# Convolution taps of six channel tiles as 32-column products in four column groups, on rows that transfers lay out four times

## The chip, the cores and the metric

The kernel runs on one core of one Trainium2 chip. The metric is the device time of one execution in microseconds; the profile is one profiled execution on that core. Engines: PE (TensorE; PEld is its weight load), DVE (VectorE), ACT (ScalarE), POOL (GpSimd), SP (SyncE, which issues all DMAs here).

## What is computed

A two-layer Conformer-like model on 256 tokens with 1024 channels, then a second block with gated recurrence, attention and 16 experts. The change lies in the convolution module of the first layer:

```python
def conv_module(h, w_pw1, w_dw, g_norm, w_pw2):
    u = h @ w_pw1
    a, b = jnp.split(u, 2, axis=-1)
    u = a * jax.nn.sigmoid(b)
    u = lax.conv_general_dilated(
        u, w_dw[:, None, :].astype(u.dtype), window_strides=(1,),
        padding=[(CONV_WIDTH - 1, 0)],
        dimension_numbers=("NWC", "WIO", "NWC"),
        feature_group_count=D_MODEL)
    u = jax.nn.silu(rmsnorm(u, g_norm))
    return u @ w_pw2
```

All is float32. Each of the 1024 channels has 31 tap weights of its own: out[c, t] is the sum over w of w_dw[w, c] u[c, t + w - 30].

## The kernel before, in words

Channels lie on partitions, in KD = 8 tiles of 128; tokens lie on the free axis, T = 256. There is one program per engine, and semaphores order them; each engine works its own list strictly in order. Weights come in 1 MB slots into a ring of six; SP issues a slot's load when the product that used the place before is done (`wait_free`).

**Products in three parts** (`split_product`, `mm3`, lines 702 to 704). A weight half slot is split into a high part by ACT (`split_hi`, line 1454) and the rest by DVE (`split_lo`, line 1958), and x likewise. There are four half-slot buffers, so ACT can split a half when the half four before it has been multiplied. PE takes 24 products per half slot.

**pw1** has eight slots in pairs: the even slot of a pair makes a, the odd one b, for two channel tiles. DVE's `glu_gate` (line 2096) multiplies b by the norm's root, ACT takes the sigmoid (line 1561), GpSimd's `scale_gate` (line 1896) multiplies by the root again (for a), and DVE's `glu` (line 2088) writes the product with a into `conv_in`, whose rows have 30 zeros ahead of them. Ahead of pw1 slot 2, PE turns the rows of the small vectors and of w_dw into columns (lines 842 to 845), and DVE copies all 248 columns of tap weights into `w_dw_room` (line 2076). ACT then computes the condition's SiLU (line 1544) and goes on with the splits.

**The taps.** Tiles 0, 1, 3, 5 and 7 are summed on DVE, 31 instructions of 256 columns each (`taps`, lines 2113 and 2117), spread by hand between the splits and GLU steps of pw1 and behind them. Tiles 2, 4 and 6 are on PE: for each tap ACT scales the identity by the column of weights (`diagonals`, line 1552, a ring of 16), and PE multiplies the 128x128 diagonal by the 256 columns of `conv_in` that begin at w (`tap`, line 873): 93 products into banks 7 and 1.

**The stage between pw1 and pw2 on PE** (list in the PE program): for each of six early chunks of the modulation, `mod_product` (line 855: for each half slot four products of 32 columns of weights, in four column groups, by 512), `turn_mod` of the chunk before (line 862), and a share of the taps (`TAP_STEPS`). Behind chunk 2 come the transposes of the context rows (line 890), behind chunk 3 the sums of the context's squares (`sum_squares`, line 734), behind chunk 5 its turn, then the sums of conv_out's squares, 22 products with zeros (`KEEP_WARM`, line 900), and pw2 with four slots. ACT copies each chunk's product (line 1574), makes diagonals, copies sums of taps out of PSUM (`take_taps`, line 1567), squares and takes the roots (line 1442). DVE takes the reciprocal (line 1929), the normed tiles (line 1938) and the low parts of x (line 1950), and pw2 begins.

SP's list: pw1's eight loads, six chunks of modulation (two loads each, `mod_chunk`), pw2's four loads, and the next feed-forward block.

Of the kernel before, what the change touches and what calls it, by code (L numbers as in the profile page):

```python
# [15 lines left out]
ALU = mybir.AluOpType  # L16
# [3 lines left out]
P = 128  # L20
D = 1024
KD = D // P
T = 256
# [14 lines left out]
KEEP_WARM = 22  # L38
# [44 lines left out]
NORMS = ("ffn0", "conv_in", "context", "conv_out", "ffn1", "ffn2", "mla", "mla_q", "mla_kv", "ffn3", "tokens", "final1")  # L83
# [8 lines left out]
PE_MARKS = ("first_gains_turned", "rows_turned", "ctx_turned", "rope_turned", "ak_product", "key_dec_turned",  # L92
# [37 lines left out]
def constant_table():  # L130
# [6 lines left out]
    }  # L137

# [25 lines left out]
    parts["mask_cols"] = np.tile(np.where(p < CHUNK, 0.0, MASKED), (P, 1))  # L164
    parts["inv_freq"] = (np.float64(10000.0) ** (-2.0 * (p % (ROPE // 2)) / ROPE))[:, None]
# [25 lines left out]
def build(nc, x, positions, ffn_norm1, ffn1_w1, ffn1_w3, ffn1_w2, mix_norm, ffn_norm2, ffn2_w1, ffn2_w3, ffn2_w2,  # L191
# [15 lines left out]
    with ExitStack() as ctx:  # L207
# [32 lines left out]
        w_dw = w_dw_room[:, 0:KD * CONV_W].rearrange("p (k w) -> p k w", w=CONV_W)  # L240
# [65 lines left out]
        conv_in, conv_acc, glu_sig = r1.take(KD, PAD + T), r1.take(KD, T), r1.take(2, 2 * T)  # L306
        cond_pad, mod_rows = r1.take(KD, 32), r1.take(2, 512)

        PE_TILES, DVE_TILES = (2, 4, 6), (0, 1, 3, 5, 7)
        DIAGS = 16  # L310
        TAP_BANK = {2: (7, 0), 4: (7, T), 6: (1, 0)}
        TAPS = [(j, w) for j in PE_TILES for w in range(CONV_W)]
        TAP_STEPS = (0, 16, 32, 47, CONV_W * 2, 78, len(TAPS))
        diag = arena[:, ARENA - 16 * P:ARENA].rearrange("p (q c) -> p q c", c=P)
# [187 lines left out]
        def _(sp):  # L502
# [26 lines left out]
            def small_inputs():  # L529
                rows_in(vectors[2:])  # L530
                sp.dma_start(rows_dw, conv_w_dw[0]).then_inc(sem("rows_in"), 16)
                for j, g in enumerate((q_norm_g_2, k_norm_g_2)):
                    for half in range(2):
                        sp.dma_start(qk_gain[64 * half:64 * half + 64, j:j + 1], g.rearrange("a d -> d a")
                                     ).then_inc(sem("gains_in"), 16)
                sp.dma_start(mask_in, masks).then_inc(sem("masks_in"), 16)
                sp.dma_start(router[:, :, :], w_router_2[0].rearrange("(k p) e -> p k e", p=P)).then_inc(sem("router_in"), 16)
                sp.dma_start(pos_i[:, :], positions.partition_broadcast(P)).then_inc(sem("positions_in"), 16)
# [54 lines left out]

            for c in range(MOD_EARLY):
                mod_chunk(c)
            for j in range(4):
# [88 lines left out]
        def _(pe):  # L685
# [42 lines left out]
            def sum_squares(m, k_tiles, n, bank, first=0):  # L728
# [1892 lines left out]
```

## Time and profile before

| what | us |
|---|---|
| median of 3 runs | 1828.26 (1827.47 to 1829.78) |
| the profiled execution, its own time | 1828.54 |
| its span | 1826.7 |
| PE busy, of the span | 1668.9 (91%) |
| DVE, ACT, POOL busy | 844.6, 684.5, 10.7 |
| mean granted clock of PE, share of full speed | 0.968 |

The span runs from the first to the last instruction of the execution; the own time is 1.84 us longer. Busy time of an engine is the union of its instructions; matmuls are pipelined, so that the duration of one (from issue to modelled end) is longer than the distance from its start to the next one's. A float32 product that is not split leaves two records. "Idle before" names the instruction that ended an engine's wait.

### The profile page before, as it was taken

The page shows a single profiled execution, that of the slowest core. Times are in us where ns is not written, and L with a number is a line of the kernel's source. Part 1 is how long each engine was busy: PE and PEld are TensorE (multiplying, and loading weights), DVE is VectorE, ACT ScalarE, POOL GpSimd, SP SyncE. Part 2 cuts the span into 40 slices and gives each one's busy share as a digit, 9 for nine tenths or more (in the row PEclk, how much of TensorE's full clock was granted, in tenths as well). Part 3 has the DMA queues.
Part 4 walks back from the last instruction along what each step waited for, and adds up shares of the span by engine and source line. Part 5 has one row for each costly group of instructions (what it writes and reads, how often), then busy time and mean ns, then how long its engine had stood idle before and what let it go on. Part 6 is the DMA issues. An engine that isn't in the chain of part 4 may idle for free.

```text
span 1826.7 us, 31145 instructions
## 1 busy us (share of the span) xinstructions
PE 1668.9 (91%) x13465; PEld 1416.3 (78%) x13465; DVE 844.6 (46%) x1201; ACT 684.5 (37%) x954; POOL 10.7 (1%) x8
## 2 busy tenths in 40 slices
PE   8999999999999999999999999999999876675755
PEld 7999997899999999868999988988786432322422
DVE  6555698765557555314655564984522000000001
ACT  5444547644445444223444455756602010100101
POOL 0000020000000000000000000000000000000000
PEclk9999999999999999999999999999999998978988
DMA  9745455355555455352554352435677999999997
GB/s 293 249 163 191 151 194 198 120 185 192 185 181 176 164 191 184 113 193 89 203 184 168 131 165 95 133 106 171 268 285 302 426 426 427 427 427 426 425 427 328
DMA packets 189679, 427.50 MB, mean 234 GB/s; under 512 B 8004, under 2 KB 146678, under 8 KB 174485
## 3 DMA queue, kind: packets, MB, share of 16 engines
q1 hardware_dynamic: 189588, 426.19, 63.5%
q8 instruction: 70, 1.15, 0.3%
q14 instruction: 21, 0.16, 0.0%
HBM read 425.12 MB, written 1.05 MB: 233 GB/s over the span
## 4 chain that ended last, share of the span: by engine, by line
PE 73%; DMA 20%; DVE 5%; ACT 1%; issue 1%; SPq 0%; another core or an unknown queue 0%; DVEq 0%; ACTq 0%
PE banks L702 15%; PE banks L704 15%; PE banks L703 15%; DMA arena<-in_w_exp_gate 5%; DMA ring<-in_w_exp_gate 3%; DMA xn<-in_w_exp_up 3%; DMA h<-in_w_exp_down 3%; DMA arena<-in_w_exp_down 3%; DMA arena<-in_w_exp_up 2%; PE banks L873 2%; DMA ring<-in_w_exp_up 2%; PE banks L1084 2%; PE banks L1086 2%; PE banks L1085 2%; PE banks L1358 2%; PE banks L825 2%
## 5 line engine op out<-in xcount | busy, mean ns | idle before, releaser
L702 PE MATMUL banks<-x_split,w_split 128*128 128x256 f32 x1600 | 456.4, 285 | 9.5 <-DVE w_split L1958 3.9
L1958 DVE TENSOR_TENSOR w_split<-ring,w_split 128x1024 fp32r<-128x1024 f32 x288 | 346.4, 1224 | 237.9 <-ACT w_split L1454 237.4
L703 PE MATMUL banks<-x_split,w_split 128*128 128x256 f32 x1600 | 452.7, 283 | 0.0
L704 PE MATMUL banks<-x_split,w_split 128*128 128x256 f32 x1600 | 452.7, 283 | 0.0
L1454 ACT ACTIVATE w_split<-ring 128x1024 fp32r<-128x1024 f32 x287 | 295.2, 1051 | 190.0 <-PE banks L704 188.2
L702 PEld LDWEIGHTS banks<-x_split,w_split 128*128 128x128 f32 x1600 | 307.0, 192 | 13.3 <-issue 5.8
L703 PEld LDWEIGHTS banks<-x_split,w_split 128*128 128x128 f32 x1600 | 307.0, 192 | 0.3
L704 PEld LDWEIGHTS banks<-x_split,w_split 128*128 128x128 f32 x1600 | 307.0, 192 | 0.0
L702 PE MATMUL banks<-hid_split,w_split 128*128 128x256 f32 x704 | 199.6, 284 | 0.0
L703 PE MATMUL banks<-hid_split,w_split 128*128 128x256 f32 x704 | 199.2, 283 | 0.0
L704 PE MATMUL banks<-hid_split,w_split 128*128 128x256 f32 x704 | 199.2, 283 | 0.0
L702 PEld LDWEIGHTS banks<-hid_split,w_split 128*128 128x128 f32 x704 | 135.1, 192 | 0.6 <-DVE hid_split L2027 0.6
L703 PEld LDWEIGHTS banks<-hid_split,w_split 128*128 128x128 f32 x704 | 135.1, 192 | 0.0
L704 PEld LDWEIGHTS banks<-hid_split,w_split 128*128 128x128 f32 x704 | 135.1, 192 | 0.0
L2582 DVE TENSOR_TENSOR roots<-banks,roots 128x256 f32<-128x256 f32 x16 | 6.8, 424 | 268.7 <-PE banks L1358 268.7
L1358 PE MATMUL banks<-arena 128*32 128x256 f32 x992 | 76.2, 462 | 37.1 <-DMA arena<-in_w_exp_up 25.3
L1358 PEld LDWEIGHTS banks<-arena 128*32 128x32 f32 x992 | 35.1, 128 | 77.1 <-DMA arena<-in_w_exp_up 31.7
L1086 PE MATMUL banks<-x_hi,w_rest 128*128 128x256 f32 (+1 forms) x288 | 89.8, 312 | 0.0
L1503 ACT ACTIVATE hid_split<-gated 128x512 fp32r<-128x512 f32 x44 | 27.8, 632 | 150.3 <-DVE gated L2025 150.3
L2012 DVE TENSOR_TENSOR gated<-banks,roots 128x512 f32<-128x512 f32 x88 | 60.3, 685 | 34.2 <-PE banks L704 34.0
L2587 DVE TENSOR_TENSOR roots<-banks,arena 128x512 f32<-128x512 f32 x16 | 11.1, 691 | 138.8 <-PE banks L1364 138.8
L1084 PE MATMUL banks<-x_hi,w_gates 128*128 128x256 f32 (+1 forms) x216 | 70.5, 327 | 0.0
(411 smaller groups left out, 2260.3 us busy)
## 6 DMA issues: line engine op xcount, KB each, us to landing
ring<-in_ffn_w SPq DMA_DIRECT2D x131, 1024.0 KB, 5.1
arena<-in_w_exp_gate SPq DMA_DIRECT2D x13, 2048.0 KB, 45.0
ring<-in_w_mod SPq DMA_DIRECT2D x24, 1024.0 KB, 5.1
arena<-in_w_exp_down SPq DMA_DIRECT2D x12, 2048.0 KB, 45.2
arena<-in_w_exp_up SPq DMA_DIRECT2D x11, 2048.0 KB, 45.7
ring<-in_w_in SPq DMA_DIRECT2D x21, 1024.0 KB, 5.2
ring<-in_w_exp_down SPq DMA_DIRECT2D x9, 2048.0 KB, 45.0
ring<-in_w_exp_gate SPq DMA_DIRECT2D x7, 2048.0 KB, 46.7
```

Source lines behind the costliest of these rows:

```text
L702: mm(out_, hi, moving(0), start=start, stop=False, **kw)
L703: mm(out_, hi, moving(1), start=False, stop=False, **kw)
L704: return mm(out_, lo, moving(0), start=False, stop=stop, **kw)
L825: last = mm(ps[:, bank0 + tile // 2, (tile % 2) * T:(tile % 2) * T + T], slot(n)[:, k * half_cols + o * P:k * half_cols + o * P + P], src[ ...
L873: mm(ps[:, b, c:c + T], diag[:, q % DIAGS, :], conv_in[:, j, w:w + T], start=(w == 0), stop=(w == CONV_W - 1)).then_inc(sem("diag_used"), 1)
L1084: mm(out_, hi, x_hi[:, k, rows], start=(k == 0), stop=False)
L1085: mm(out_, hi, x_rest[:, k, rows], start=False, stop=False)
L1086: last = mm(out_, lo, x_hi[:, k, rows], start=False, stop=(k == KD - 1))
L1358: last = mm(ps[32 * q:32 * q + 32, 4 + m, 0:256], src(2 * j + k), w[:, k * D + 256 * q:k * D + 256 * q + 256], start=(j == 0 and k == 0), ...
L1454: fn(half_part(n, o, 0), half_slot(n, o, columns), ACT.Copy).then_inc(sem("half_hi"), 1)
L1958: ins = dve.tensor_tensor(half_part(n, o, 1), half_slot(n, o, columns), half_part(n, o, 0).bitcast(F32), ALU.subtract)
L2012: return dve.tensor_tensor(dst, ps[:, bank + c % 2, :].rearrange("p (k t) -> p k t", t=T), scale, ALU.mult)
```

## The change

Tiles 0 and 1 stay on DVE. Tiles 2 to 7 go to PE, two at a time. For a pair of tiles SP issues 16 SBUF to SBUF transfers (`shift_pair`): for each of four row groups g of 32 channels and each shift `first` of 0 to 3 columns, the 32 rows go to partitions 32*first, so that each group of channels lies on all 128 partitions, four times, each time a column further on. One product then does four taps of 32 channels; eight of them (m), 4 columns apart, do all 31 taps. The four groups of channels are the four column groups. DVE makes the weights, 128x1024 a tile, from a table `quad` and the tap weights (`spread_taps`); ACT lays the tap weights out as `w_tap`, in 16 small copies from PSUM. GpSimd's part goes; DVE scales both a and b by the root (`glu_scale`), and pw1's slots 4 and 6 wait for that rather than for glu. PE waits for all four glu ahead of the first modulation product. conv_out's sums go ahead of modulation product 5 and of the context's sums; the context's root moves behind conv_out's on ACT and DVE; the last turn goes between pw2 slots 1 and 2; the warming products fall from 22 to 4. `conv_acc` lies where the normed tiles will be (`xn[:, :, T:2T]`), and pairs 1 and 3 share the rows of `conv_in`. Several semaphores of small loads become one, `small_in`.

```diff
-KEEP_WARM = 22
+KEEP_WARM = 4
...
+    quad = p[:, None] % 32 == np.arange(32)[None, :]
...
-        w_dw = w_dw_room[:, 0:KD * CONV_W].rearrange("p (k w) -> p k w", w=CONV_W)
+        w_dw = w_dw_room[:, 0:2 * CONV_W].rearrange("p (k w) -> p k w", w=CONV_W)
+        w_tap = w_dw_room[:, 64:256].rearrange("p (k g m) -> p k g m", g=4, m=8)
...
+            def shift_pair(p):
+
+                sp.wait_ge(sem("glu_ready"), p + 1)
+                for first in range(4):
+                    for g in range(4):
+                        sp.dma_start(shifted[p][32 * first:32 * first + 32, :, g, :],
+                                     conv_pair(p)[32 * g:32 * g + 32, :, first:first + WIDE]
+                                     ).then_inc(sem(f"pair_shifted_{p}"), 16)
+
             for c in range(MOD_EARLY):
                 mod_chunk(c)
+                if c < 3:
+                    shift_pair(c + 1)
...
                 if j >= 4 and j % 2 == 0:
-                    pe.wait_ge(sem("glu_ready"), j // 2 - 1)
+                    pe.wait_ge(sem("glu_scaled"), j // 2 - 1)
...
+            def taps(pair):
+
+                pe.wait_ge(sem(f"pair_shifted_{pair}"), 16 * 16)
+                for a in range(2):
+                    j = 2 * pair + a
+                    pe.wait_ge(sem("taps_spread"), j - 1)
+                    for m in range(8):
+                        for g in range(4):
+                            last = mm(ps[32 * g:32 * g + 32, PAIR_BANK[pair], a * T:a * T + T],
+                                      tap_room(j)[:, g, 32 * m:32 * m + 32], shifted[pair][:, a, g, 4 * m:4 * m + T],
+                                      start=(m == 0), stop=(m == 7))
+                last.then_inc(sem("pe_mark"), 1)
...
+            pe.wait_ge(sem("cond_ready"), 1)
+            pe.wait_ge(sem("glu_ready"), KD // 2)
+            early_mod(0)
+            taps(1)
+            early_mod(1)
+            taps(2)
+            early_mod(2)
+            pe.wait_ge(sem("taps_copied"), 1)
+            taps(3)
+            early_mod(3)
             pe.wait_ge(sem("taps_copied"), 2)
+            pe.wait_ge(sem("ctx_in"), 16)
...
+            early_mod(4)
+            sum_squares("conv_out", KD, T, 7)
+            early_mod(5)
+            sum_squares("context", KD, T, 4, at=T)
+            pe.wait_ge(sem("mod_copied"), 5)
             for _ in range(KEEP_WARM):
...
             for j in range(4):
                 split_product(FIRST["pw2"] + j, j, first="pw2" if j == 0 else None)
+                if j == 1:
+                    pe.wait_ge(sem("std_ready"), NORM["context"])
+                    turn_mod(MOD_EARLY - 1, mod_rows, 4, T + 8 * (MOD_EARLY - 1))
...
+            rows = ps[:, 6, 2 * CONV_W:KD * CONV_W].rearrange("p (k w) -> p k w", w=CONV_W)
+            for first in range(4):
+                n = 8 if first < 3 else 7
+                for g in range(4):
+                    fn(w_tap[32 * first:32 * first + 32, :, g, 0:n],
+                              rows[32 * g:32 * g + 32, :, first:first + 4 * n - 3:4], ACT.Copy)
...
+            mod_copy(0, mod_rows, 5)
+            take_taps(1)
+            mod_copy(1, mod_rows, 6)
+            take_taps(2)
+            mod_copy(2, mod_rows, 5)
+            take_taps(3)
+            mod_copy(3, mod_rows, 6)
+            act.wait_ge(sem("conv_done"), 2)
+            for pair in range(4):
+                square_pair(pair)
...
+            fn(xn[:, :, 0:T], ctx_rows, ACT.Copy).then_inc(sem("ctx_copied"), 1)
+            mod_copy(4, mod_rows, 5)
+            fn(squares[:, :, T:2 * T], ctx_rows, ACT.Square).then_inc(sem("squares_ready"), 1)
+            split_hi_slot(FIRST["pw2"])
+            root("conv_out", 7, D)
...
+            def glu_scale(pair):
+
+                wait_done(dve, FIRST["pw1"] + 2 * pair + 1)
...
+                dve.tensor_tensor(glu_sig[:, pair % 2, :].rearrange("p (a t) -> p a t", t=T),
+                                  ps[:, (2 * pair + 1) % 4, :].rearrange("p (a t) -> p a t", t=T), scale, ALU.mult
+                                  ).then_inc(sem("glu_gate_scaled"), 1)
+                if pair == 3:
+                    dve.wait_ge(sem("pair_shifted_1"), 16 * 16)
+                dve.tensor_tensor(conv_pair(pair)[:, :, PAD:PAD + T],
+                                  ps[:, (2 * pair) % 4, :].rearrange("p (a t) -> p a t", t=T), scale, ALU.mult
+                                  ).then_inc(sem("glu_scaled"), 1)
...
+                dve.tensor_tensor(tap_room(j).rearrange("p g (m c) -> p g m c", c=32),
+                                  const("quad").unsqueeze(1).unsqueeze(1).to_broadcast([P, 4, 8, 32]),
+                                  w_tap[:, j - 2].unsqueeze(3).to_broadcast([P, 4, 8, 32]), ALU.mult
+                                  ).then_inc(sem("taps_spread"), 1)
...
+            glu_scale(0)
             split_lo_slot(FIRST["pw1"] + 4)
             glu(0)
             taps((0, 0, 4), (1, 0, 4))
             split_lo_slot(FIRST["pw1"] + 5)
-            glu_gate(1)
-            taps((0, 4, 8), (1, 4, 8))
+            glu_scale(1)
+            taps((0, 4, 6), (1, 4, 6))
             glu(1)
+            spread_taps(2)
+            spread_taps(3)
             split_lo_slot(FIRST["pw1"] + 6)
-            taps((0, 8, 12), (1, 8, 12))
+            taps((0, 6, 9), (1, 6, 9))
             split_lo_slot(FIRST["pw1"] + 7)
-            glu_gate(2)
-            taps((0, 12, 17), (1, 12, 17))
+            spread_taps(4)
+            glu_scale(2)
+            taps((0, 9, 11), (1, 9, 11))
             glu(2)
-            taps((0, 17, 24), (1, 17, 24))
-            glu_gate(3)
-            taps((0, 24, CONV_W), (1, 24, CONV_W), (3, 0, 6))
+            spread_taps(5)
+            taps((0, 11, 16), (1, 11, 16))
+            glu_scale(3)
+            taps((0, 16, 18), (1, 16, 18))
             glu(3)
-            taps((3, 6, CONV_W), (5, 0, 20))
-            taps((5, 20, CONV_W), (7, 0, 12))
-            taps((7, 12, CONV_W))
-            root("context", T)
+            spread_taps(6)
+            spread_taps(7)
+            taps((0, 18, CONV_W), (1, 18, CONV_W))
             split_lo_slot(FIRST["pw2"])
-            dve.wait_ge(sem("taps_copied"), len(PE_TILES))
+            dve.wait_ge(sem("taps_copied"), 3)
             normed("conv_out", x_in, conv_acc, gains("conv_norm"))
             x_lo("pw2")
             split_lo_slot(FIRST["pw2"] + 1)
+            root("context", T)
             split_lo_slot(FIRST["pw2"] + 2)
```

## Rows read from the trace of the kernel before

**Rows 1.** The page, part 4: the chain that ended last, by engine.

```profile
PE 73%; DMA 20%; DVE 5%; ACT 1%; issue 1%; SPq 0%; another core or an unknown queue 0%; DVEq 0%; ACTq 0%
```

**Rows 2.** Windows, 259 to 326: start:end, us, busy of each engine, PEclk, DMA share, GB/s.

```profile
259.00:326.00 67.00, 67.00 (x382) 50.78 (x383) 55.64 (x125) 45.04 (x99) 1.27 (x1) 1.00 0.60 201
```

**Rows 3.** Timeline of PE: start, us, engine, line, operation [idle before, releaser].

```profile
258.93 1.92 PE L855 MATMUL banks<-ring,arena 128*32 128x512 f32 x16
260.78 7.18 PE L873 MATMUL banks<-arena 128*128 128x256 f32 x32
267.89 1.92 PE L855 MATMUL banks<-ring,arena 128*32 128x512 f32 x16
269.75 1.05 PE L862 MATMUL banks<-consts,arena 128*128 128x2 f32 x8
270.66 7.16 PE L873 MATMUL banks<-arena 128*128 128x256 f32 x32
...
321.79 3.70 PE L734 MATMUL banks<-squares,consts 128*128 128x256 f32 x16
325.32 4.91 PE L900 MATMUL banks<-zero_w 128*128 128x512 bf16 x22
331.89 0.36 PE L702 MATMUL banks<-x_split,w_split 128*128 128x256 f32 x1 [1.66 <-DVE x_split L1950]
```

**Rows 4.** Timeline of PE in the experts: products of 128x32 weights.

```profile
1411.96 1.91 PE L1358 MATMUL banks<-arena 128*32 128x256 f32 x32
1413.69 1.91 PE L1358 MATMUL banks<-ring,arena 128*32 128x256 f32 x32
```

**Rows 5.** Timeline of ACT, pw1 slot 2.

```profile
220.78 0.22 ACT L1544 ACTIVATE arena<-vec_b 128x16 f32<-128x16 f32 x1 [1.25 <-DVE w_dw_room L2076]
220.91 2.94 ACT L1454 ACTIVATE w_split<-ring 128x1024 fp32r<-128x1024 f32 x3
```

**Rows 6.** Timeline of DVE in pw1 and behind it.

```profile
229.05 1.54 DVE L1958 TENSOR_TENSOR w_split<-ring,w_split 128x1024 fp32r<-128x1024 f32 x1 [1.65 <-ACT w_split L1454]
...
236.39 2.35 DVE L1958 TENSOR_TENSOR w_split<-ring,w_split 128x1024 fp32r<-128x1024 f32 x2
...
258.48 5.62 DVE L2117 SCALAR_TENSOR_TENSOR arena<-arena,w_dw_room 128x256 f32<-128x256 f32 x14
264.01 0.68 DVE L2096 TENSOR_TENSOR arena<-banks,roots 128x512 f32<-128x512 f32 x1
...
273.51 0.67 DVE L2088 TENSOR_TENSOR arena<-banks,arena 128x512 f32<-128x512 f32 x1
```

**Rows 7.** Timelines of ACT and DVE, the conv_out root up to pw2.

```profile
289.02 1.88 ACT L1583 ACTIVATE xn<-banks 128x2048 f32<-128x2048 f32 x1 [1.34 <-PE banks L890]
...
325.52 0.47 ACT L1442 ACTIVATE roots<-banks,eps_col 128x256 f32<-128x256 f32 x1 [3.24 <-PE banks L734]
326.01 1.28 ACT L1605 ACT_TABLE_LOAD   x1
...
326.10 1.75 DVE L1929 RECIPROCAL roots<-roots 128x256 f32<-128x256 f32 x1 [4.14 <-ACT roots L1442]
327.89 3.26 DVE L1938 SCALAR_TENSOR_TENSOR xn<-arena,vec_a,roots 128x256 f32<-128x256 f32 x8
331.06 1.88 DVE L1950 TENSOR_TENSOR x_split<-xn,x_split 128x512 fp32r<-128x512 f32 x3
```

**Rows 8.** Timeline of SP's queue: issues of small transfers.

```profile
20.84 0.25 SPq L522 DMA_DIRECT2D arena<-in_mla_kv_norm  x1
...
24.70 1.20 SPq L534 DMA_DIRECT2D qk_gain<-in_q_norm_g  x2
```

**Rows 9.** DMA issues, 195 to 368 us: size, median us to landing.

```profile
ring<-in_w_mod SPq DMA_DIRECT2D x12, 1024.0 KB, 5.3
```

**Rows 10.** Timeline of PE in the experts, a product behind a gap.

```profile
1498.98 3.33 PE L1358 MATMUL banks<-xn,arena 128*32 128x256 f32 x32 [2.86 <-DMA xn<-in_w_exp_gate]
```

**Rows 11.** Windows view behind two gaps in the experts, columns as in rows 2.

```profile
1455.00:1457.00 2.00, 1.97 (x12) 0.68 (x16) 0.00 (x0) 0.00 (x0) 0.00 (x0) 0.50 0.98 418
```

More of the change, by code:

```diff
@@ L305, in build, with conv_pair, tap_room @@
         PAD = CONV_W - 1
[L306 to L314, printed above, removed]
+        WIDE = T + CONV_W - 3
+        conv_in, glu_sig = r1.take(6, PAD + T + 1), r1.take(2, 2 * T)
+        shifted_1, shifted_2 = r1.take(2, 4, WIDE), r1.take(2, 4, WIDE)
+        cond_pad = r1.take(KD, 32)
+        mod_rows = gated[:, 0, :].rearrange("p (r c) -> p r c", r=2)
+        conv_acc = xn[:, :, T:2 * T]
+        CONV_PLACE = (0, 1, 2, 1)
+        def conv_pair(p):
+            return conv_in[:, 2 * CONV_PLACE[p]:2 * CONV_PLACE[p] + 2, :]
+        x_room = arena[:, LOW + HALF_BUFS * SLOT:LOW + HALF_BUFS * SLOT + 2 * KD * T]
+        shifted_3 = x_room[:, 0:8 * WIDE].rearrange("p (k g t) -> p k g t", k=2, g=4)
+        shifted = {1: shifted_1, 2: shifted_2, 3: shifted_3}
+        def tap_room(j):
+            if j in (2, 3):
+                room = arena[:, ARENA - 2048 + 1024 * (j - 2):ARENA - 2048 + 1024 * (j - 1)]
+            elif j in (4, 5):
+                return squares[:, 4 * (j - 4):4 * (j - 4) + 4, T:2 * T]
+            else:
+                room = x_room[:, 8 * WIDE:8 * WIDE + 1024] if j == 6 else gated[:, 1, :]
+            return room.rearrange("p (g n) -> p g n", g=4)
+        PAIR_BANK = {1: 7, 2: 0, 3: 7}
         mod_rows_late = tok[:, 0, :].rearrange("p (r c) -> p r c", r=2)
@@ L733, in sum_squares @@
                         pe.wait_ge(sem("squares_ready"), SQ_BEFORE[m] + i // per + 1)
-                    last = mm(ps[:, bank, 0:n], ones[:, 0:P], squares[:, first + i, 0:n],
+                    last = mm(ps[:, bank, 0:n], ones[:, 0:P], squares[:, first + i, at:at + n],
                               start=(i == 0), stop=(i == k_tiles - 1))
@@ L1592, in _, with square_pair @@
-            act.wait_ge(sem("conv_done"), 3)
-            act.wait_ge(sem("taps_copied"), 2)
-            square(conv_acc[:, 2:4, :], 2, T)
-            act.wait_ge(sem("conv_done"), 4)
-            square(conv_acc[:, 4:6, :], 4, T)
-            take_taps(2, 1)
-            act.wait_ge(sem("conv_done"), 5)
-            act.wait_ge(sem("taps_copied"), 3)
-            square(conv_acc[:, 6:8, :], 6, T)
-            root("conv_out", 4, D)
+            def square_pair(pair):
+                if pair > 0:
+                    act.wait_ge(sem("taps_copied"), pair)
+                square(conv_acc[:, 2 * pair:2 * pair + 2, :], 2 * pair, T)
@@ L1606, in _ @@
                 fn(x_g, x_g, ACT.Silu).then_inc(sem("x_hi"), 1)
+            root("context", 4, D, region=T)
+            split_hi_slot(FIRST["pw2"] + 1)
+            mod_copy(5, mod_rows, 6)
             split_hi_slot(FIRST["pw2"] + 2)
@@ L1920, in _ @@
             dve.memset(cond_pad, 0.0)
+            dve.memset(w_dw_room[:, :], 0.0)
             dve.memset(eps_col[:, :], EPS)
```

127 lines of the change are left out of this document (38 added, 89 removed).

## The prediction

> **What bounds the kernel now.** I read the chain of waits on the page first: PE is 73% of it and DMA 20%, and the DMA share lies at the end, in the experts [rows 1]. The change touches one stage of layer 0, from the last quarter of the pw1 product to the start of the pw2 product. The windows view of that stage is next: from 259 to 326 us PE is busy the whole 67 us at granted clock 1.00, its 2.4 GHz level, DVE 55.6 us, ACT 45.0 us [rows 2]. So PE's queue sets the time there, and PE's timeline shows what stands in it [rows 3]: one early modulation product (1.85 us from its start to the next one's), 16 taps (7.11 us, from start to start), again and again, then the conv_out sums at 321.79, the 22 warming products at 325.32, and pw2 at 331.89. There are 93 taps, each with two records, so six such batches. Behind pw1 everything waits for this queue, and what follows pw2 isn't edited apart from semaphore names, so I take a microsecond saved before pw2 as one saved at the end.
>
> **PE's removals.** Old: 93 products of 128x128 by 256. New: three pairs of 64 products of 128x32 by 256, four column groups at a time. The expert products have exactly this shape: 32 records, which are 16 products, start 1.73 us after the 16 before them [rows 4], so 64 take 6.9 us and three pairs 20.7. A modulation product, eight 512-column products in four groups, takes 1.85 us, by which a pair would be 7.4; nothing in the trace runs faster than 6.9, so that is the lower end, and the upper is 64 x 0.44 = 28 us, if the groups took turns. I take 6.9, the row of the same shape. Old, by the 7.11 us of 16: 93 x 0.444 = 41.3. Gain on PE: 41.3 - 20.7 = 20.6 us. Here the Trainium skill (TensorE: Matmul & The Clock Gate, Part 3: Packing small matmuls) is less kind: four-fold packing measured 3.07 times as fast, which would make a pair about 9 us and the sum 6 us smaller. The expert rows come out near 4 times, and the sum goes by them.
>
> **The order behind the taps.** The conv_out sums move ahead of modulation product 5, turn 4 and the context sums. Before, all of these stood ahead of them; now they run while the conv_out root goes through ACT and DVE, where the 22 warming products stood. That takes 1.85 + 0.91 + 3.6 (as the conv_out sums, 3.5 to 3.7 [rows 3]) = 6.3 us off the path. Turn 5 moves between pw2 slots 1 and 2 and costs there what it saves: nothing net. Warming falls from 22 to 4: no cost, it filled a wait.
>
> **Added ahead of slot 2 on ACT.** The 16 copies into w_tap stand after the condition's SiLU at 220.78, ahead of the pw1 slot 2 split, which started at 220.91 [rows 5]. They have 48 elements on 32 partitions; the nearest row is that SiLU, 0.22 us long for 16 elements, and back to back ACT starts the next 0.13 us later. I take 0.17 each, 2.7 us; ends 0.1 and 0.3. PE had about 1 us of cover on that split (DVE's low part ended about 223.2, PE wanted it at 224.2), so PE stands still 1.7 us at slot 2 (0.6 to 3.8). This delays DVE's chain by as much.
>
> **DVE becomes the bound in pw1, the new wait.** PE now waits for all four GLU pairs ahead of modulation product 0. Before, it didn't: glu(3) ended at 274 [rows 6] and only the context transposes wanted it. I add up DVE's list. The first low split of slot 4 was at 229.05 [rows 6]; with the late slot 2, and the sigmoid ahead of it on ACT, I put it at 231.6. From there to the end of glu(3) DVE issues 8 low splits at 1.14 (two take 2.35), 36 taps at 0.40 (14 take 5.53 [rows 6]) plus 0.3 for the first, 3 glu_scale calls of two instructions and 4 glu at 0.60 each (a 512-element operation, as the x_split low parts: three in 1.88 [rows 7]), 4 spread_taps of 1024 elements at 1.14 (as the low split, same element count and width), and 0.3 of waits: 9.1 + 14.7 + 3.6 + 2.4 + 4.6 + 0.3 = 34.7, so 266.4. Spread_taps reads both inputs with repeats, which no row shows; bounds 0.6 (a cheaper form, as the 512-element one) and 2.3 (twice the split), I take the split. PE ends pw1 at 258.9 + 1.7 = 260.6 and starts product 0 at 266.6 where it started at 258.93: 7.7 us lost. GpSimd's four multiplies leave the path to each glu; DVE pays for them in the glu_scale calls counted above.
>
> **SP's queue.** 48 shift transfers of 73 KB. Issue: 0.25 us for a small load, 0.60 for a transfer of 64 pieces [rows 8]; each shift has 64 pieces of 1136 bytes; I take 0.35 to 0.40. Landing: 5.3 us for a 1 MB load [rows 9], so at most that; I take 2.2. Queued behind a pair's waits and 16 issues are the modulation loads, and behind those the next pair. Pair 1: glu(1) at 244, landed by 252. Pair 2: 258, landed 266. Pair 3: 266.6, landed 275, wanted by PE at 288 (266.6 plus three modulation products, two turns and two pairs). Modulation chunk 2 is issued at 264, wanted at 285. All hidden: 0. glu_scale(3) on DVE also waits for pair 1 to be in (its rows are written over), 12 us after it landed: 0. In exchange the chunk 1 loads come 15 us later than before; they are wanted at 275: 0.
>
> **The end of the stage.** ACT has, after the copy of modulation product 3 at about 296.9: that copy, four squares, context copy, copy 4, context square, the pw2 slot 0 split, a table load (1.28), the root: 0.5 + 2.2 + 1.8 + 0.5 + 1.8 + 1.9 + 1.28 + 0.4 = 10.4 (2048 elements take 1.9, a load 1.28 [rows 7]), so the root ends at 307.3, while the sums on PE end at 266.6 + 3 x 6.9 + 5 x 1.85 + 4 x 0.95 + 1.8 + 3.5 = 305.6. Before, the root came right after the sums. From root to pw2 as before: reciprocal 1.76, eight norms 3.26, first low part 0.6, in all 5.9 from root end to PE [rows 7]. Pw2 starts at 313.3, a microsecond more of tail than before. Sum: -20.6 - 6.3 + 7.7 + 1.0 = -18.2; laid out event by event I get 313.3 against 331.9 for the start and -17.6 for the end of pw2 (turn 5 is inside it now), and take -17.6.
>
> **The clock.** PE's wait from 260.6 to 266.6 is longer than any it has in this stage. After 2.86 us of idling an expert product of 32 records took 3.33 us for 1.91 [rows 10], and a window behind such gaps has granted clock 0.50, the 1.2 GHz level [rows 11]. So I charge one such stretch, +1.7 us (0 if it stays up, 3.4 for two). The Trainium skill (TensorE: Matmul & The Clock Gate, Part 1) says that an idle PE is put to half rate until it has been busy again; by that rule, the trace agrees.
>
> The profiled execution took 1828.54 us (span 1826.7), the median of the runs is 1828.26, 0.3 less. 1828.54 - 17.6 + 1.7 = 1812.6; against the median 1812.4.
>
> **Rivals.** (a) Forecast, taps four abreast and shifts hidden: 1812.4, chance 0.76. Its own range goes from 1808.5 (no clock loss, w_tap copies at 0.1) to 1817 (0.3 per copy, +2; two clock stretches, +1.7; tap rounds at the modulation product's rate, +1.5).
> (b) DVE carries more than I added up: the spreads cost twice a split. Four of them stand ahead of glu(3), +4.6 us: 1817. For: two repeated inputs; against: the element count and type are the split's. Chance 0.12.
> (c) Slower. The shifts are the bound: 48 issues and their landings in one queue, from glu(1) at 244. They have to be in by 288; with 1.5 us of loads and 2.2 to land, each may take (288 - 244 - 3.7) / 48 = 0.84 us. Past it each 0.1 us costs 4.8 us, the gain is gone at 1.17 us each, and at 1.3 us the time is 1812.4 + 48 x 0.46 = 1834.5. For: SP's rows reach 0.60, and no row shows a transfer from SBUF to SBUF; against: most small issues take 0.25. Chance 0.06. The Trainium skill (DMA: Bandwidth & Descriptors, Rules for kernel authors) speaks for this rival: coalesce small transfers, since near 64 KB one pays mostly overhead. No run here shows it for these.
> (d) The change doesn't do what it says: with a weight load for each 32 columns and two different operands per group, the column groups take turns. Then 3 x (28 - 6.9) = 63 us more: 1876. The expert products also load weights each time and don't take turns [rows 4]. Chance 0.02.
> (e) No net change: shifts at 1.15 us each, or stalls of 12 us that I don't see, chance 0.04: 1828.
>
> **Range and chances.** (a) and (b) hold 0.88; the range 1807.5 to 1820 takes them in with the bounds of the copies, the clock and the tap rate. About 0.2% (3.7 us) is what a measurement can tell from no change. Faster by more: (a), (b) and a little of (e), 0.89; within: 0.04; slower: 0.07.
>
> **What would show it.** Right: 128 records of 128x32 taps in about 6.9 us per pair; an idle PE of about 6 us ahead of the first modulation product, ended by DVE's glu; a stall of 1 to 2 us at pw1 slot 2, ended by a split; SP's shifts 0.4 us apart; pw2 starting near 313 to 315. Wrong: PE waiting for DMA ahead of a pair of taps, spreads much longer than 1.2 us, a PE stretch at 0.5 longer than 4 us, or a wait between the conv_out sums and pw2 of over 9 us.

## The result, and the profile after

| | before | after |
|---|---|---|
| median, run side by side | 1827.91 (4 runs) | 1813.01 (4 runs, 1812.48 to 1817.31) |
| the profiled execution | 1828.54 | 1813.03 |
| its span | 1826.7 | 1811.2 |

The ratio is 0.992 (0.9907 to 0.9932), 14.9 us faster by the medians, where 15.9 were forecast. The page of the changed kernel, first line of busy times and the chain by engine (against 73% in [rows 1]):

```profile
PE 1646.9 (91%) x13645; PEld 1391.5 (77%) x13645; DVE 813.9 (45%) x1120; ACT 657.7 (36%) x879; POOL 0.2 (0%) x4
...
PE 71%; DMA 21%; DVE 5%; ACT 2%; issue 1%; DVEq 0%; SPq 0%; ACTq 0%
```

The shares of the chain have hardly moved, and DVE has 5% as before. What did move is in PE's timeline of the stage (start, us, line, operation; in brackets the idle time before and its releaser):

```profile
227.85 0.38 PE L734 MATMUL banks<-x_split,w_split 128*128 128x256 f32 x1 [2.06 <-DVE w_split L1987]
...
268.08 3.64 PE L887 MATMUL banks<-ring,arena 128*32 128x512 f32 x16 [5.42 <-issue]
271.46 7.33 PE L906 MATMUL banks<-arena 128*32 128x256 f32 x128
...
281.42 7.12 PE L906 MATMUL banks<-arena,squares 128*32 128x256 f32 x128
288.36 1.90 PE L887 MATMUL banks<-ring,arena 128*32 128x512 f32 x16
...
291.17 3.66 PE L906 MATMUL banks<-arena 128*32 128x256 f32 x64
...
305.49 3.70 PE L766 MATMUL banks<-squares,consts 128*128 128x256 f32 x16
309.12 1.92 PE L887 MATMUL banks<-ring,arena 128*32 128x512 f32 x16
...
311.89 3.70 PE L766 MATMUL banks<-squares,consts 128*128 128x256 f32 x16
315.43 1.03 PE L942 MATMUL banks<-zero_w 128*128 128x512 bf16 x4
...
318.11 0.36 PE L734 MATMUL banks<-x_split,w_split 128*128 128x256 f32 x1 [1.66 <-DVE x_split L1979]
```

Read it against [rows 3]. PE stands still 2.06 us at pw1 slot 2; it ends pw1 at 262.7, waits for DVE ("issue" here is the wait for the last glu), and starts modulation product 0 at 268.08. That one takes 3.4 us to the start of the taps where it took 1.85. Then 128 records of 128x32 taps take 6.94 us from start to start, and pw2 starts at 318.11 instead of 331.89. The windows view gives the clock of the two stretches around product 0 (columns as in [rows 2]):

```profile
264.00:268.00 4.00, 0.00 (x0) 0.00 (x0) 4.00 (x10) 0.63 (x1) 0.00 (x0) 0.64 1.04 195
268.00:272.00 4.00, 3.92 (x24) 1.23 (x28) 4.00 (x7) 0.23 (x1) 0.00 (x0) 0.51 0.62 129
```

DVE's timeline (first two rows: spread_taps, then glu(3), which ends PE's wait; the last three belong to the end of the stage):

```profile
245.70 2.36 DVE L2142 TENSOR_TENSOR arena<-consts,w_dw_room 128x1024 f32<-128x1024 f32 x2
...
267.27 0.70 DVE L2134 TENSOR_TENSOR arena<-arena 128x512 f32<-128x512 f32 x1
...
308.06 1.22 DVE L1987 TENSOR_TENSOR w_split<-ring,w_split 128x1024 fp32r<-128x1024 f32 x1 [27.51 <-ACT w_split L1499]
311.18 1.23 DVE L1987 TENSOR_TENSOR w_split<-ring,w_split 128x1024 fp32r<-128x1024 f32 x1 [1.90 <-PE banks L887]
312.32 1.75 DVE L1958 RECIPROCAL roots<-roots 128x256 f32<-128x256 f32 x1
```

ACT's timeline, the 16 copies into w_tap, the split of pw2's slot 0 and the conv_out root:

```profile
222.08 3.38 ACT L1595 ACTIVATE w_dw_room<-banks 32x48 f32<-32x48 f32 x16
...
306.97 2.00 ACT L1499 ACTIVATE w_split<-ring 128x1024 fp32r<-128x1024 f32 x2
...
310.28 0.48 ACT L1487 ACTIVATE roots<-banks,eps_col 128x256 f32<-128x256 f32 x1
```

SP's timeline, the three pairs' transfers, and the row of the DMA issues view with their size and median time to landing:

```profile
245.82 10.72 SPq L620 DMA_DIRECT2D arena<-arena  x16
...
259.53 10.27 SPq L620 DMA_DIRECT2D arena<-arena  x16
...
271.08 11.26 SPq L620 DMA_DIRECT2D arena<-arena  x16
...
arena<-arena SPq DMA_DIRECT2D x48, 71.0 KB, 3.7
```

16 issues take 10.3 to 11.3 us: 0.67 us each, and 3.7 us to land.

**How the 15.5 us of span come about.** One offset has to be taken out first. Slot 1 of the first product, long before anything that the change touches on PE, starts at 28.55 us in the profile of before and at 29.89 in this one: in its first 20 us the granted clock is 0.91 and not 1.00. (Nine of the ten profiles below have the late start too, and one, that with 15 warming products, does not, with the same code there. So it is no fixed cost of the code; whether the change makes it likelier, the one profile of before can't tell.) The changed kernel reaches the stage 1.34 us late. The next feed-forward product behind pw2 starts at 357.07 before and at 344.17 after: 12.9 us, and without the offset 14.2. The rest comes later and isn't the change's. Before's profile has a half-clock stretch in the second mixer that after's lacks there; the same group of 96 products takes 22.64 us in one and 20.96 in the other. Before:

```profile
750.46 22.64 PE L920 MATMUL banks<-xn,ring 128*128 128x256 f32 x96 [0.39 <-DVE xn L1938]
```

```profile
752.00:756.00 4.00, 4.00 (x13) 3.21 (x12) 0.77 (x3) 0.00 (x0) 0.00 (x0) 0.59 0.64 243
```

After:

```profile
737.60 20.96 PE L965 MATMUL banks<-xn,ring 128*128 128x256 f32 x96 [0.39 <-DVE xn L1967]
```

That is 1.7 us. 14.2 - 1.3 + 1.7 = 14.6, and the 0.9 us that are left lie further on; I didn't follow them.

### The profile page after: what moved, and what is told of

It reads as the page before. It is cut to its first block, busy times and chain, and to the rows that moved or that the text cites. A ratio compares the mean times of both kernels' runs of the same rounds, so it can differ in the third digit from the quotient of the medians.

```text
span 1811.2 us, 31390 instructions
## 1 busy us (share of the span) xinstructions
PE 1646.9 (91%) x13645; PEld 1391.5 (77%) x13645; DVE 813.9 (45%) x1120; ACT 657.7 (36%) x879; POOL 0.2 (0%) x4
## 4 chain that ended last, share of the span: by engine, by line
PE 71%; DMA 21%; DVE 5%; ACT 2%; issue 1%; DVEq 0%; SPq 0%; ACTq 0%
PE banks L734 15%; PE banks L736 15%; PE banks L735 15%; DMA xn<-in_w_exp_up 5%; DMA arena<-in_w_exp_down 5%; DMA h<-in_w_exp_down 3%; DMA squares<-in_w_exp_gate 3%; DMA arena<-in_w_exp_up 2%; DMA ring<-in_w_exp_up 2%; PE banks L1129 2%; PE banks L1131 2%; PE banks L1130 2%; PE banks L1403 2%; PE banks L857 2%; PE banks L1273 2%; PE banks L1307 1%
```

## The experiments

All are edits of the changed kernel. The kernel before ran beside them, nine times in each of three batches, with medians of 1828.05 us (the first three below and copies (a)), 1827.51 (copies (b), DVE's order, the cut transfers, all mends) and 1828.58 (15 warming products, the root's order); the ratios go by these. By their ratios only all mends and the root's order are clear of the changed kernel's interval on the fast side; the first and the cut transfers, one run each, are far clear on the slow side. For the rest the rows of one profile each speak, not the times.

**Do the column groups run side by side, and why?** The loops over m and g change places, so that eight products of one column group follow each other.

```diff
-                    for m in range(8):
-                        for g in range(4):
+                    for g in range(4):
+                        for m in range(8):
```

> The same 192 products of 32 columns, but the eight products of one column group follow one another before the next group begins (loops over g and m exchanged). My theory (the 20.6 us gained on PE come from four groups running side by side, which needs neighbours in different groups): a tile takes 32 x 0.43 = 13.8 us where it took 3.5, a pair 27.6 instead of 7.0, and the time rises by about 62 us to 1875. Rival (the gain comes from fewer or cheaper products as such, 192 of 32 columns for 93 of 128, and the order is of no matter): the time stays at 1813. Anything between says that groups overlap at their seams only: with three of four seams a pair near 26 us.

Measured: 1857.42 us, one run. PE's timeline, the second pair:

```profile
296.06 21.34 PE L906 MATMUL banks<-arena,squares 128*32 128x256 f32 x125
```

A pair takes 21.0 us for 6.94 from its start to that of the next product, three times as long, though it is the same 64 products on the same data: 42 of the 44 us lost. So it is the order of the groups that lets them run together. The expected 28 us a pair were too many: inside a group the products start 0.43 us apart, as expected, but at each seam the last two of one group run beside the first two of the next, so that a group of eight takes 2.62 us.

**Is the wait for all four glu the cost in front, and do the transfers bear an earlier start?** PE waits for three glu only, which is what product 0 and pair 1 need.

```diff
-            pe.wait_ge(sem("glu_ready"), KD // 2)
+            pe.wait_ge(sem("glu_ready"), KD // 2 - 1)
```

> PE waits for three GLU pairs instead of four ahead of modulation product 0, so nothing holds it at the end of pw1. My theory (the wait for glu(3) costs 5.5 us of standing still and 1.7 us of half clock, and the shifts have about 5 us of slack before taps of pair 3): product 0 starts at 262.6 instead of 268.1 and takes 1.9 us, so PE gains 7.2 us; then the taps of pair 3 want their rows at about 284, while the last of them lands at about 286, which gives 2 us back. Time about 5.2 us less than the changed kernel, 1807.8. Rival (the wait only hides another, the shifts of pair 2 or 3 bind at once): 1811 to 1813.

Measured: 1815.63 us (ratio 0.9935, 0.9921 to 0.9949), no gain at all. The profile is of the fastest of the five runs, 1810.60; the others took 1815.46 to 1817.59. PE's timeline:

```profile
262.90 1.92 PE L887 MATMUL banks<-ring,arena 128*32 128x512 f32 x16
...
286.45 6.52 PE L906 MATMUL banks<-arena 128*32 128x256 f32 x64 [2.27 <-issue]
...
317.25 0.36 PE L734 MATMUL banks<-x_split,w_split 128*128 128x256 f32 x1 [2.66 <-DVE x_split L1979]
```

Product 0 starts 5.2 us earlier and takes its full-clock 1.92 us. But now pair 3 waits 2.27 us for its transfers, which land when they did before, and behind that wait half of the pair (64 records) takes 6.5 us where it took 3.66. The 5.2 us go back in one place, 2.3 in the wait and 2.9 in the low clock behind it. What is left over there, 1.9 us, is what the changed kernel loses to the clock at product 0, and 1.0 of it goes in the longer wait ahead of pw2 (last row), where ACT's split of pw2's slot 0 waits 2.35 us for its load. That answers what the last wait of the stage is: if PE doesn't wait for DVE, it waits for SP's queue. The forecast's slack of 13 us on pair 3 was 5. Why the median is 2.6 us above that of the changed kernel, this profile of the fastest run can't show; it stays open.

**What does the clock cost?** 24 zero products stand ahead of the wait for glu(3).

```diff
+            for _ in range(24):
+                mm(banks(7, 1), zero_w[:, 0:P], zero_w[:, :], start=True, stop=True)
             pe.wait_ge(sem("glu_ready"), KD // 2)
```

> 24 products with zeros (128x512, bf16, 0.215 us each, 5.2 us) stand ahead of PE's wait for the four GLU pairs; nothing else is altered. My theory: they fill the 5.5 us wait, the granted clock stays at 1.00, modulation product 0 takes 1.9 us instead of 3.64 and the first taps 6.9 instead of 7.1, so the time is 1.7 us less, 1811.3, with the start of product 0 unmoved. Rival (the slow first product is the cost of starting on column groups or of something else than the clock): no change, 1813.0.

Measured: 1813.35 us (0.9896 to 0.9923), single runs from 1808.98 to 1814.40. PE's timeline:

```profile
264.62 5.35 PE L921 MATMUL banks<-zero_w 128*128 128x512 bf16 x24
270.14 1.92 PE L887 MATMUL banks<-ring,arena 128*32 128x512 f32 x16 [0.17 <-DVE arena L2136]
```

DVE's, glu(3):

```profile
269.40 0.69 DVE L2136 TENSOR_TENSOR arena<-arena 128x512 f32<-128x512 f32 x1
```

Product 0 takes 1.92 us behind them, and with pair 1 it takes 8.65 us to the start of the next product, where the changed kernel took 10.52: the 1.9 us of low clock are gone. The warming delayed nothing, since glu(3) ended at 270.09, behind the last of it. Product 0 starts 2.1 us later than in the changed kernel because pw1 ended 2.1 us later (264.8): this execution was 0.6 us late before slot 2 and lost 1.5 us behind the 2.03 us stall there, with clock 0.62 from 228 to 232 us. The medians don't separate it from the changed kernel; the rows separate the mechanism.

**The copies into w_tap.** First behind the splits of slots 2 and 3 (a), then between the splits of slots 4 and 5, with the first spreads waiting for them (b). Both move this block on ACT; (b):

```diff
                     split_hi_slot(FIRST["pw1"] + 2 * i + 2)
+                    if i == 1:
+                        ...
+                                fn(w_tap[32 * first:32 * first + 32, :, g, 0:n],
+                                   rows[32 * g:32 * g + 32, :, first:first + 4 * n - 3:4], ACT.Copy)
                     split_hi_slot(FIRST["pw1"] + 2 * i + 3)
```

> ACT's 16 small copies into w_tap stand behind the splits of pw1 slots 2 and 3 instead of ahead of them. My theory (they cost PE 2.06 us at slot 2 and start DVE's chain as much later, and DVE's chain sets the end of glu(3)): no stall at slot 2, glu(3) about 2.3 us earlier, PE's wait unchanged at about 5.5 us, time 1810.7. Rival (the delay at slot 2 is swallowed by the later wait for glu(3)): PE's wait grows by 2 us and the time stays 1813.0.

> The 16 copies into w_tap stand between the splits of pw1 slots 4 and 5. With them behind slot 3 the stall at slot 2 went, but glu(3) came only 0.7 us earlier, since the sigmoid of pair 0 and the split of slot 4 stood behind the copies. My theory: here neither does, slot 4's first low split starts near 230.5 instead of 233.4, and glu(3) is 2.7 us earlier; PE ends pw1 at 260.4 and waits 4.8 us; time 1810.3, and the runs lie closer together than those of the changed kernel, since the 2 us stall at slot 2 put the clock at risk. Rival (another wait takes its place, as before): glu(3) earlier by under 1 us, time 1812.

Measured: 1811.53 (0.9894 to 0.9924) and 1812.05 us (0.9898 to 0.9925). PE's timeline of (a), then of (b):

```profile
267.41 3.64 PE L887 MATMUL banks<-ring,arena 128*32 128x512 f32 x16 [6.95 <-issue]
```

```profile
266.34 3.64 PE L887 MATMUL banks<-ring,arena 128*32 128x512 f32 x16 [5.42 <-issue]
269.72 8.31 PE L906 MATMUL banks<-arena 128*32 128x256 f32 x128
```

The stall at slot 2 is gone in both, and pw1 ends 2 us earlier, but PE only waits longer for glu(3) (6.95 us for 5.42): in (a) the copies delay the sigmoid and the high split of slot 4 instead, so DVE is late all the same, and product 0 gains 0.7 us; in (b) it gains 1.7. Only 0.8 of these 1.7 us reach modulation product 1, because the low clock lasts further into pair 1 (8.1 us from start to start, for 7.1 in the changed kernel). PE's stall itself was hidden behind DVE's list; what the copies cost is the delay of ACT's splits, and by them of that list. What the stall does do is to put the clock at risk: seven profiles have it, at 2.03 to 2.06 us, and two of them (warm wait, and the cut transfers below) have a clock of 0.62 and 0.58 from 228 to 232 us, the other five 1.00. Four runs of (a) lie within 1.4 us, those of the changed kernel within 4.8.

**DVE's order.** glu(3) goes ahead of five of the seven rounds of taps that stood between glu(2) and it.

```diff
-            taps((0, 11, 16), (1, 11, 16))
+            taps((0, 11, 13), (1, 11, 13))
             glu_scale(3)
-            taps((0, 16, 18), (1, 16, 18))
             glu(3)
+            taps((0, 13, 18), (1, 13, 18))
```

> On DVE, ten of the fourteen taps of tiles 0 and 1 that stood ahead of glu(3) (3 of 5 behind glu(2), all 2 pairs between glu_scale(3) and glu(3)) move behind it. My theory (PE's wait at the end of pw1 is DVE's own list, nothing else): glu_scale(3) starts when pw1 is done, at 262.5, glu(3) ends at 264.4 instead of 267.9, product 0 starts 3.5 us earlier, the idle is 2 us; if the clock stays up, 1.7 us more. Time 1809.5, or 1807.8 with the clock. Rival (glu(3) would wait for another anyway: the sigmoid, or pair 1's transfers, whose rows it writes over): product 0 near 268, time 1813.

Measured: 1814.04 us (0.9914 to 0.9941): no gain, though in its profile pw2 starts 2.5 us earlier. PE's timeline:

```profile
312.04 1.03 PE L942 MATMUL banks<-zero_w 128*128 128x512 bf16 x4
...
315.62 0.35 PE L734 MATMUL banks<-x_split,w_split 128*128 128x256 f32 x1 [2.55 <-DVE x_split L1979]
...
318.89 0.41 PE L736 MATMUL banks<-x_split,w_split 128*128 128x256 f32 x1
```

The last row is one of the second product group: behind 2.55 us of idling, pw2's products start 0.21 us apart instead of 0.12, for 16 of them. That gives 1.5 of the 2.5 us back, and the next feed-forward product starts 1.0 us earlier than in the changed kernel. Product 0 starts at 264.88, as the theory had it, but behind 2.29 us of idling it lost the clock too. So in this execution the four warming products that the change left are too few. They aren't in every one: the early start's profile has 2.66 us of idling in the same place, and pw2 keeps its 0.12 us behind them. It was put to the test by itself, with 15 of them on top of this kernel:

```diff
-KEEP_WARM = 4
+KEEP_WARM = 15
```

> The kernel with glu(3) ahead of the taps on DVE, and with 15 warming products ahead of pw2 where it had 4. In its profile pw2 started 2.5 us earlier than in the changed kernel, but behind an idle PE of 2.55 us its first 18 products ran 0.21 us apart for 0.12, which gave 1.7 us back. Theory (that clock loss ate the gain): 11 more products of 0.22 us fill the 2.55 us, pw2's first products stay 0.12 us apart, and the median falls from 1814.0 to about 1812.3, or 1811.3 with the whole 2.5. Rival (the gain was lost later on, in SP's loads or behind): 1814 as before, with pw2 at full clock.

Measured: 1812.29 us (0.9905 to 0.9933), single runs from 1809.13 to 1816.54. PE's timeline:

```profile
310.76 3.19 PE L942 MATMUL banks<-zero_w 128*128 128x512 bf16 x14
...
314.20 0.36 PE L734 MATMUL banks<-x_split,w_split 128*128 128x256 f32 x1 [0.25 <-DVE x_split L1979]
```

The idle time is filled, pw2's products start 0.12 us apart, and from pw2's start to the next feed-forward product it takes 26.0 us for 27.5 without them: the 1.5 us. The median is 1.75 us lower, as expected; the runs spread too widely to call the 1.75 itself shown. The rows show the mechanism. The forecast had said that fewer warming products cost nothing.

**The price of a transfer.** Each of the 48 is cut in two, one tile each: 96 issues of half as many pieces for the same bytes.

```diff
-                        sp.dma_start(shifted[p][32 * first:32 * first + 32, :, g, :],
-                                     conv_pair(p)[32 * g:32 * g + 32, :, first:first + WIDE]
-                                     ).then_inc(sem(f"pair_shifted_{p}"), 16)
+                        for a in range(2):
+                            sp.dma_start(shifted[p][32 * first:32 * first + 32, a, g, :],
+                                         conv_pair(p)[32 * g:32 * g + 32, a, first:first + WIDE]
+                                         ).then_inc(sem(f"pair_shifted_{p}"), 16)
```

> Each of the 48 shift transfers is cut in two, one channel tile each: 96 of 32 pieces, the same bytes. An issue of 64 pieces took 0.67 us. If that is a price per piece: 0.34 us each, a pair 10.7 us as before, time 1813. If it is a price per transfer: 0.6 us or more each, a pair over 19 us; then glu_scale(3) waits for pair 1 (to about 269), pair 3 is issued from 290 to 311, its taps start near 315 instead of 291, and the time rises by about 25 us to 1838. That second case is also my rival (c) brought about on purpose: by its sum (48 issues at 1.3 us or so) the time would be 1834.5 or a little over.

Measured: 1840.87 us, one run. SP's timeline, then PE's:

```profile
247.43 21.48 SPq L621 DMA_DIRECT2D arena<-arena  x32
...
270.13 20.77 SPq L621 DMA_DIRECT2D arena<-arena  x32
...
292.12 20.73 SPq L621 DMA_DIRECT2D arena<-arena  x32
```

```profile
273.22 3.64 PE L888 MATMUL banks<-ring,arena 128*32 128x512 f32 x16 [8.95 <-issue]
...
292.21 9.07 PE L907 MATMUL banks<-arena,squares 128*32 128x256 f32 x128 [4.54 <-DMA arena<-arena]
...
314.25 6.53 PE L907 MATMUL banks<-arena 128*32 128x256 f32 x64 [10.28 <-issue]
...
345.80 0.36 PE L735 MATMUL banks<-x_split,w_split 128*128 128x256 f32 x1 [3.40 <-DVE x_split L1980]
```

32 issues take 20.7 to 21.5 us: 0.65 to 0.67 each, with half the pieces. The price is one per transfer. And this is rival (c) brought about: every step now waits for transfers (product 0, because glu_scale(3) needs pair 1 to be in; pair 2, 4.5 us; pair 3, 10.3 us), and the kernel is slower than before. At 0.67 us each, 48 transfers leave 5 us of slack; 96 cost 28 us, of which a part is low clock behind these waits (pair 1 takes 8.2 us and pair 2 8.9 for 6.9).

**All mends together.** PE's start behind the third GLU pair, glu(2), as in the early start, copies (b), glu(3) ahead of spread_taps(5) and five taps, half of the transfers of pairs 2 and 3 from ACT's queue, and the second low split of pw2's slot 0 behind the low parts of x:

```diff
-                for first in range(4):
+                for first in range(4 if p not in (2, 3) else 2):
                     for g in range(4):
                         sp.dma_start(shifted[p][32 * first:32 * first + 32, :, g, :],
...
+            def shift_half(p):
+                act.wait_ge(sem("glu_ready"), p + 1)
+                for first in range(2, 4):
+                    for g in range(4):
+                        act.dma_start(shifted[p][32 * first:32 * first + 32, :, g, :],
+                                      conv_pair(p)[32 * g:32 * g + 32, :, first:first + WIDE]
+                                      ).then_inc(sem(f"pair_shifted_{p}"), 16)
...
-            split_lo_slot(FIRST["pw2"])
+            split_lo(FIRST["pw2"], 0)
...
             x_lo("pw2")
+            split_lo(FIRST["pw2"], 1)
```

> All together: w_tap copies between the splits of slots 4 and 5, taps of tiles 0 and 1 behind glu(3), PE waits for three GLU pairs ahead of product 0, half of the transfers of pairs 2 and 3 issued by ACT, and on DVE the second half of pw2 slot 0's low split behind the low parts of x (it stood ahead of the conv_out reciprocal and waits for modulation product 5). My theory adds the waits of the changed kernel's trace: no idle PE from pw1 to the conv_out sums, so product 0 at 260.5, taps of pair 3 at 282 (their rows in at about 273), sums end 300, root 301.4, pw2 at 307.3 instead of 318.1, time 1802. Rival (transfers in two queues share the same engines and land no earlier, so pair 3's rows come at 280 or later, PE idles and the clock falls): 1807 or more.

Measured: 1805.12 us (ratio 0.9878, 0.9863 to 0.9893). ACT's issues and SP's beside each other, then PE:

```profile
265.20 6.50 ACTq L1598 DMA_DIRECT2D arena<-arena  x8
...
265.20 5.76 SPq L620 DMA_DIRECT2D arena<-arena  x8
```

```profile
272.40 1.05 PE L894 MATMUL banks<-consts,gated 128*128 128x2 f32 x8 [1.22 <-ACT gated L1627]
```

At the same time, SP issues eight in 5.8 us and ACT eight in 6.5 (0.72 and 0.81 each, a little more than one queue alone), and pair 3 is no longer waited for. The new wait is 1.22 us ahead of turn 0, whose copy stands behind ACT's issues. The Trainium skill (DMA: Bandwidth & Descriptors, Rules for kernel authors) says that spreading transfers over engines brings no bandwidth and saves only the time that issuing takes; here the time of issuing was the bound, and this run agrees that it can be saved; on bandwidth no run here says anything. Pw2 started at 309.6, 2.3 us later than expected, because ACT's split of pw2's slot 0 waited for its load and the root waited behind it.

**The order in front of the root.** On top of that: ACT copies product 0 before it issues, and conv_out's root stands ahead of the split of pw2's slot 0, whose low part goes behind the normed tiles.

```diff
-            shift_half(3)
             mod_copy(0, mod_rows, 5)
+            shift_half(3)
...
-            split_hi_slot(FIRST["pw2"])
             root("conv_out", 7, D)
+            split_hi_slot(FIRST["pw2"])
```

> The version with all mends again, with two orders changed. ACT copies modulation product 0 before it issues its half of pair 3's transfers, so the 1.22 us for which turn 0 waited go; and conv_out's root stands ahead of the split of pw2's slot 0 on ACT (that split waited 0.88 us for its load and took 2.0), with the low split behind the normed tiles on DVE. Theory (the tail is set by what stands ahead of the root): the sums end near 299.8, a table load of 1.28 and the root of 0.47 end at 301.6 instead of 303.7, reciprocal 1.75, norms 3.26, low split 1.2: pw2 starts near 308.8 instead of 309.6 and the time is 1804.3; if the table load goes in while ACT waits, pw2 starts at 307.5 and the time is 1803.0. Rival (pw2's own loads bound the tail): pw2 starts at 309.6 or later, 1805.1.

Measured: 1803.04 us (0.9845 to 0.9875), runs from 1802.55 to 1803.98: 25.5 us less than before, and about 10 less than the change. ACT's timeline, then PE's:

```profile
297.96 1.28 ACT L1487 ACT_TABLE_LOAD   x1
300.10 0.47 ACT L1487 ACTIVATE roots<-banks,eps_col 128x256 f32<-128x256 f32 x1 [0.85 <-PE banks L766]
300.52 2.00 ACT L1499 ACTIVATE w_split<-ring 128x1024 fp32r<-128x1024 f32 x2
```

```profile
306.51 0.81 PE L942 MATMUL banks<-zero_w 128*128 128x512 bf16 x3
307.60 0.36 PE L734 MATMUL banks<-x_split,w_split 128*128 128x256 f32 x1 [0.28 <-DVE x_split L1992]
```

The table load goes in while ACT would wait (297.96), the root comes 0.1 us behind the sums, the split stands behind it at no cost, and pw2 starts at 307.60, 2.0 us earlier than with all mends. That is the better of the two branches expected. The intervals of the two ratios overlap, so the 2 us rest on these rows.

## Why the prediction was right

The time came out 0.6 us from the forecast, and the mechanism is the forecast one: four groups abreast on PE, PE waiting for glu(3), one loss of clock, transfers hidden. By its own steps, with the 1.3 us offset taken off after's times:

- **Taps at the expert products' rate**: a pair takes 6.94 us, forecast 6.9. The row of the same shape was the right one. The Trainium skill's 3.07 times (TensorE: Matmul & The Clock Gate, Part 3), which the page has for four row groups and 512 columns, would by an estimate have given 9 us a pair. Measured on these column groups of 256, against 64 x 0.444, it is 4.1 times.
- **PE's wait for glu(3)**: product 0 starts at 266.7, forecast 266.6. The stall at slot 2 was 2.06 us, not 1.7 (copies of 0.21 us, not 0.17), PE's end of pw1 came 0.7 us later than forecast, and the wait was 5.4 us, not 6.0. DVE's list began 0.5 us late as well (232.1 for 231.6) but took 34.5 us to the end of glu(3), not 34.7, and the 266.4 written for its end were a slip for 266.3; so the hit to 0.1 us is in part luck. Spread_taps took 1.13 us each, forecast 1.14, so rival (b) is out. As the copies' runs show, the stall was no loss of its own.
- **The clock**: product 0 and the first of its followers cost 1.9 us more than in the warm wait's profile, forecast 1.7, with the granted clock at 0.51 from 268 to 272 us, its 1.2 GHz level. The forecast looked for this only ahead of product 0. It didn't see that the cut to four warming products leaves the wait ahead of pw2 open to the same loss, which the changed kernel escaped with 1.66 us of idling and the kernel with glu(3) first didn't with 2.55.
- **SP's queue**: right in its result, wrong in its terms. Issue was taken at 0.35 to 0.40 us, between rows of 0.25 and 0.60 for transfers from HBM [rows 8]; it is 0.67, above the upper bound. Landing was taken at 2.2 us; it is 3.7. So pair 3 lands about 285, wanted at 290, where 275 and 288 were forecast. Rival (c)'s threshold of 0.84 us was the useful number: 0.67 lies under it, but it was far nearer than a chance of 0.06 says. The Trainium skill's rule named at that rival (DMA: Bandwidth & Descriptors, Rules for kernel authors) is for transfers under 64 KB, and these have 71. For the cut ones, half as large, the trace agrees with it: 0.65 to 0.67 us each, as much as a whole one.
- **The end of the stage**: this is the term that was mis-sized. Root at 309.4 against 309.0 by the forecast with its clock term; but pw2 starts at 316.8 against 315.0. The DVE row at 311.18 has the 1.5 us: the second low split of pw2's slot 0 waits for modulation product 5, which the change has moved behind the conv_out sums, and the reciprocal stands behind that split on DVE. It needs nothing that the product makes: the split is counted on the same semaphore (`slot_free`), so it has to come behind it. The forecast counted what the move frees on PE, and put this wait at nothing. With the split behind the low parts of x (all mends) the way from the root's end to pw2 took 5.9 us, as in the kernel before; here it took 7.4.

Sum in the stage: 14.2 us gained at the start of the next product, forecast 17.6 - 1.7 = 15.9; the missing 1.7 is that split (1.5) and small terms. That the time came within 0.6 us is closer than the stage was, and luck: the two profiled executions differ by as much outside the stage (-1.3 and +1.7). Rival (d) fell with the 6.94 us, and (e) with it.

Not settled: what the runs of one kernel differ by (up to 5 us) is half-clock stretches of some 1.5 us at several places as far as the profiles show it, but no run was made for that alone.

## What to carry to other kernels

When a step leaves the critical engine, add up issue and landing of every transfer that takes its place, by a row of the same kind, and if there is none measure one: here 48 transfers between two places in SBUF at 0.67 us each became the bound when PE came to them 5 us earlier. When a product is moved on one engine, look for who on the others waits for the semaphore that it counts on, and what is queued behind them. And a wait that gets a little longer can cost more than its length by the clock behind it, so warming products are cut only once the wait that is left is known.

## What the runs showed of the hardware that had not been expected

- A transfer of 71 KB within SBUF costs SP 0.67 us to issue, with 64 pieces and with half as many; two queues at once, 0.72 on SP and 0.77 to 0.81 on ACT.
- 128x32 products run four abreast only when neighbours in the queue belong to different column groups: 0.108 us each then, 0.33 with eight of a group in a row.
- PE's clock fell to its 1.2 GHz level behind idle times of 5.42 us (after), 2.55 and 2.29 us (glu(3) first, ahead of pw2 and of product 0), 2.27 us (early start, pair 3) and 2.03 us (warm wait, slot 2). It did not behind 1.66 and 2.06 us (after), 2.66 us (early start, ahead of pw2) or 3.40 us (cut transfers, ahead of pw2; clock 1.00 from 345 to 349 us). From 2 to 3.4 us both happen, so one profile doesn't say what a wait of that length costs in the next.
- What such a fall costs isn't fixed either: 1.5 us (warm wait, slot 2; glu(3) first, pw2), 1.9 (after, product 0 and pair 1), and 2.9 (early start, pair 3; copies (b), product 0 and pair 1, behind the same 5.42 us of idling as in after).
